# Two transformer blocks in one kernel: another way to the head norms, other places for gains, first scores, rank strips and small loads

## The chip, the cores and the metric

One NeuronCore of a Trainium2 chip. The metric is the device time of the kernel in microseconds, the median of several runs. Matmuls have float32 data; where the text says "product", it is one of three terms (hi by hi, hi by lo, lo by hi) of a split float32 product.

## What is computed

Two blocks, one after the other, on x of 512 tokens by 1024. Only the first is touched by the change. Cut to what matters:

```python
h = rms_norm(x, g_norm)
proj = h @ w_in          # q_a k_a v_a q_i k_i w_i z_a c_q c_kv k_rope z_b q_m z_m gates
q_a = partial_rope(rms_norm(q_a.reshape(b, s, 8, 64), g_qn_a), cos_a, sin_a)   # k_a likewise, g_kn_a
o_a = dsa_attention(q_a, k_a, v_a, q_i, k_i, w_i)       # an indexer picks the best 128 keys per query
q_b = (rms_norm(c_q, g_cq) @ w_uq).reshape(b, s, 8, 96)
kv_b = (rms_norm(c_kv, g_ckv) @ w_ukv).reshape(b, s, 8, 128)
k_b = concatenate([k_nope, broadcast(k_rope)])
q_b, k_b = rms_norm(q_b, g_qn_b), rms_norm(k_b, g_kn_b)  # then rotate the last 32 of 96
o_b = causal_attention(q_b, k_b, v_b)
kv_m = rms_norm(mem, g_mem) @ w_mem_kv                   # mem: 256 rows
k_m, q_m = rms_norm(k_m, g_kn_m), rms_norm(q_m, g_qn_m)  # 4 heads of 128
o_m = softmax(q_m k_m / sqrt(128)) v_m
ys = [o_a * silu(z_a), o_b * silu(z_b), o_m * silu(z_m)]
x = x + (sum_n sigmoid(gates_n) * (ys_n @ w_branch_n)) @ w_out
```

The second block (pool mixer, sparse attention, MLP of 4096) follows and takes the time from about 700 us on.

## The kernel before, in words

**Strips and pairs.** The large products run in strips on TensorE (PE). A strip has 4 PSUM banks and takes its weights in pairs: 2 x 128 rows of up to 512 columns. SP loads a pair into one of 4 ring slots (`raw`) once the pair four before is used (`load`, L457 on), ACT makes the high part (`part_hi`, L1356), POOL the low part (`split`, L606), PE uses it in `strip_products` (L777). Before each of the eight steps kt of a strip, PE may do small work given as `before` (transposes of 128x128 pieces, called groups, and first scores). A group takes a bank that the group two before it has been emptied from, by ACT ("A"), DVE ("D") or both, as `GROUPS` says; cq and ckv are "AD".

**Order of strips.** Strips 0 to 5, 7, 8, 10, 11 are the ten of `w_in` (`in1(0)` to `in1(9)`, 484 columns), strips 6 and 9 the two of the memory (512 columns, two token tiles, 4 x 12 products), 12 is gate strip 0, then stage a of attention, 13 and 14 the q ranks (`STRIP_UQ`), 15 and 16 the kv ranks (`STRIP_UKV`), 17 gate strip 1, stages b0, b1, m, and the merge strips. Each engine's program is written out by hand in this order; nothing is planned at run time.

**Start.** ACT issues the load of the identity and nine loads of small vectors into `vec_rows` (L1351), PE turns them (L726) into `vec`, then turns x (`turn_x`, four pieces at first), ACT makes xt_hi (L1385), DVE xt_lo. ACT then issues nine more small loads (L1471 to L1477) and only then the first w_hi (L1356).

**Head norms.** DVE squares and reduces q_a and k_a (L1951, L1952), forms the mean (L1969), POOL raises it to -0.5 (`inv_sqrt`, L600), DVE multiplies by the factor (L1958) and by the gain (L1959) and rotates. The same follows for the memory keys, ranks and q_m, with a second POOL power. For branch b the factor comes from ACT's root and a Newton step on DVE (`roots` L1639, `over_rms` L2270 to L2274), for all 8 heads at once behind both kv strips. POOL has the power between `split`s in its program.

**The place of the waits.** In in1(9), PE's `a_columns` at kt 2 waits for `z_ready` 2 and `qk_ready`; at kt 6 it turns z_a. In gate strip 0, `b_columns` turns z_b at kt 1 and z_m at kt 3 (`turn_z`, 16 transposes), waits for `cq_ready` at kt 5 and turns the ranks at kt 5 to 7; scores of units 0 and 1 follow. `silu(n)` (L2104) is DVE's, after ACT's tanh (`gate_tanh`, L1447). After the strip DVE scales the four gate banks (`scale_gates1`, L2256), and PE waits for it (`strip_scaled`) before the attention stage. DVE's program has silu(2) and two head scalings ahead of the low parts of the cq and ckv groups (L2249).

**Attention.** A stage works in steps of two units (a head and a block of 128 queries). Per step: scores (PE, L839), mask and maximum (DVE, L2168), exponential (ACT, L1590), reciprocal (DVE, L2189), scaling (POOL, L639), transposes (PE, L974) `LAG_T` steps later, copies (DVE L2196 for even units, ACT L1602 for odd ones), product with v (PE, L982). `AHEAD` is the number of steps whose scores stand before the stage.

**Behind stage m**, ACT copies o_a's part to ys_hi (L1707), DVE subtracts it (L2386, ys_lo), and the merge strips start.

## Time and profile before

| | |
|---|---|
| runs | 1604.28 us median of 3 (1604.19 to 1605.44) |
| the profiled execution's own time | 1605.06 us |
| its span | 1603.2 us |
| granted clock, mean | 0.969 |

The profile is of one execution. The page gives busy times of the engines over the span, the span in 40 slices, the chain of waits that ended last, and groups of instructions by line; further views give PE's instructions in order of time with the idle time ahead of each and what ended it, a table of waits, and the busy time and granted clock in chosen stretches. A busy share says little here: what counts is where PE stands, and what it stands for. "PE bank L777 x12" is twelve products of a strip.

### The profile page before, as it was taken

How to read it: one execution, taken by the hardware profiler on the slowest of the kernel's cores; microseconds unless marked ns; L12 is line 12 of the kernel's file. 1: busy time of each engine (PE TensorE's matmuls, PEld its weight loads, DVE VectorE, ACT ScalarE, POOL GpSimd, SP SyncE). 2: the span in 40 equal slices, each digit the busy share in tenths (PEclk: the TensorE clock that was granted, in tenths of full speed). 3: DMA queues.
4: the chain of work that ended last, by engine and by line, in shares of the span. 5: the costliest groups of instructions: out<-in, count | busy, mean ns of one | idle time of the engine just before them, and what ended most of it. 6: DMA issues, size and time to landing. Idle time of an engine off the chain costs nothing.

```text
span 1603.2 us, 20921 instructions
## 1 busy us (share of the span) xinstructions
PE 1510.6 (94%) x7906; PEld 1251.9 (78%) x7906; DVE 675.1 (42%) x1382; ACT 601.5 (38%) x1081; POOL 672.3 (42%) x448
## 2 busy tenths in 40 slices
PE   5999977999787999999999889999999999999998
PEld 4888866858556888889988677877888888888886
DVE  2336959564654122410316536565122333323324
ACT  3454431556355132333223527465322422222222
POOL 2433575434341344444333226353444444444443
PEclk8999998999998999999999979899999999999999
DMA  5222332102100323336522200002222222322322
GB/s 170 87 77 87 115 114 63 55 16 83 49 1 1 92 92 105 113 118 199 153 83 66 66 27 2 1 2 79 94 101 94 89 99 92 103 94 92 104 92 92
DMA packets 72426, 130.70 MB, mean 82 GB/s; under 512 B 5961, under 2 KB 28818, under 8 KB 72338
## 3 DMA queue, kind: packets, MB, share of 16 engines
q1 hardware_dynamic: 69968, 127.01, 24.7%
q10 hardware_dynamic: 2370, 2.50, 0.5%
q8 instruction: 58, 0.95, 0.2%
q14 instruction: 30, 0.25, 0.1%
HBM read 125.29 MB, written 4.19 MB: 81 GB/s over the span
## 4 chain that ended last, share of the span: by engine, by line
PE 88%; DVE 4%; ACT 3%; POOL 2%; issue 2%; DMA 1%; ACTq 0%; DVEq 0%; POOLq 0%
PE bank L777 68%; PE bank L982 4%; PE bank L839 4%; PE bank L974 4%; PE bank L726 3%; PE bank L992 1%; PE bank L841 1%; PE bank L1150 1%; POOL w_lo L606 1%; POOL rstd L600 1%; ACT w_hi L1356 1%; PE bank L1014 0%; PE bank L1315 0%; DMA vec_rows<-in_pe_v 0%; DVE q_parts L2064 0%
## 5 line engine op out<-in xcount | busy, mean ns | idle before, releaser
L606 POOL TENSOR_TENSOR w_lo<-raw,w_hi 128x1024 fp32r<-128x1024 f32 (+3 forms) x222 | 528.1, 2381 | 740.3 <-ACT w_hi L1356 740.3
L1356 ACT ACTIVATE w_hi<-raw 128x1024 fp32r<-128x1024 f32 (+3 forms) x222 | 226.5, 1023 | 640.8 <-DMA raw<-in_w_ff 255.0
L777 PE MATMUL bank<-w_hi,xt_hi 128*128 128x484 f32 (+2 forms) x640 | 242.2, 378 | 18.3 <-POOL w_lo L606 18.3
L777 PE MATMUL bank<-w_lo,xt_hi 128*128 128x484 f32 (+2 forms) x640 | 238.8, 373 | 0.0
L777 PE MATMUL bank<-w_hi,xt_lo 128*128 128x484 f32 (+2 forms) x640 | 238.7, 373 | 0.0
L777 PE MATMUL bank<-xt_hi,w_hi 128*128 128x512 f32 x576 | 227.0, 394 | 1.0 <-issue 1.0
L777 PE MATMUL bank<-xt_hi,w_lo 128*128 128x512 f32 x576 | 224.6, 390 | 0.0
L777 PE MATMUL bank<-xt_lo,w_hi 128*128 128x512 f32 x576 | 224.5, 390 | 0.0
L777 PEld LDWEIGHTS bank<-w_hi,xt_hi 128*128 128x128 f32 x640 | 121.7, 190 | 34.4 <-issue 19.7
L777 PEld LDWEIGHTS bank<-w_hi,xt_lo 128*128 128x128 f32 x640 | 121.5, 190 | 15.2
L777 PEld LDWEIGHTS bank<-w_lo,xt_hi 128*128 128x128 f32 x640 | 121.8, 190 | 14.3
L777 PEld LDWEIGHTS bank<-xt_hi,w_hi 128*128 128x128 f32 x576 | 108.3, 188 | 23.4 <-issue 1.7
L777 PEld LDWEIGHTS bank<-xt_hi,w_lo 128*128 128x128 f32 x576 | 108.2, 188 | 22.7
L777 PEld LDWEIGHTS bank<-xt_lo,w_hi 128*128 128x128 f32 x576 | 108.3, 188 | 22.2 <-issue 0.5
L777 PE MATMUL bank<-w_hi,ys_hi 128*128 128x512 f32 x240 | 93.5, 390 | 0.0
L777 PE MATMUL bank<-w_hi,ys_lo 128*128 128x512 f32 x240 | 93.5, 389 | 0.0
L777 PE MATMUL bank<-w_lo,ys_hi 128*128 128x512 f32 x240 | 93.5, 389 | 0.0
L1590 ACT ACTIVATE sc<-sc,negmax 128x128 f32<-128x128 f32 (+3 forms) x112 | 56.6, 506 | 64.2 <-DVE negmax L2168 64.0
L726 PE MATMUL bank<-cst,proj 128*128 128x128 f32 (+2 forms) x368 | 54.9, 294 | 26.0 <-issue 10.2
L2517 DVE SCALAR_TENSOR_TENSOR proj<-bank,r_rows 128x512 f32<-128x512 f32 x32 | 19.9, 684 | 140.8 <-PE bank L777 140.8
L726 PEld LDWEIGHTS bank<-cst,proj 128*128 128x128 f32 (+2 forms) x368 | 45.2, 148 | 35.7 <-issue 27.1
L2356 DVE TENSOR_TENSOR proj<-proj,bank 128x512 f32<-128x512 f32 x56 | 34.7, 682 | 69.7 <-PE bank L777 69.7
(335 smaller groups left out, 2412.9 us busy)
## 6 DMA issues: line engine op xcount, KB each, us to landing
raw<-in_w_ff SPq DMA_DIRECT2D x64, 512.0 KB, 3.5
raw<-in_w_in SPq DMA_DIRECT2D x40, 512.0 KB, 3.4
raw<-in_w_in SPq DMA_DIRECT2D x40, 484.0 KB, 3.4
raw<-in_w_in SPq DMA_DIRECT2D x24, 392.0 KB, 3.3
raw<-in_w_out SPq DMA_DIRECT2D x16, 512.0 KB, 3.6
raw<-in_w_branch SPq DMA_DIRECT2D x12, 512.0 KB, 3.6
raw<-in_w_mem_kv SPq DMA_DIRECT2D x8, 512.0 KB, 3.6
raw<-in_w_proj_nsa SPq DMA_DIRECT2D x8, 512.0 KB, 3.5
```

Of the source, the lines that this page charges most:

```text
L600: pool.tensor_tensor(rstd[:, 0:n], stat[:, 0:n], half[:, 0:n], ALU.pow).then_inc(sem["pow_done"], 1)
L606: pool.tensor_tensor(w_lo[:, slot, 0:halves, 0:width], raw[:, slot, 0:halves, 0:width], w_hi[:, slot, 0:halves, 0:width].bitcast(F32), ALU ...
L726: ins = pe.transpose(b[0:m, o:o + k], src, ident[0:k, 0:k])
L777: ins = pe.matmul(o, lhs, rhs, start=st and j == 0, stop=en and j == 2)
L839: ins = pe.matmul(o, w["q"], w["k"], start=True, stop=w["k_lo"] is None)
L841: ins = pe.matmul(o, w["q"], w["k_lo"], start=False, stop=True)
L974: ins = pe.transpose(bank[2 + u % 2][0:n, t * P:(t + 1) * P], src[:, t * P:t * P + n], ident)
L982: ins = pe.matmul(bank[4 + w["pas"] % 2][w["rows"], w["cols"]], w["v"][t], src[0:n, t * P:(t + 1) * P], start=w["start"] and t == 0, stop= ...
L1356: act.activation(w_hi[:, slot, 0:halves, 0:width], raw[:, slot, 0:halves, 0:width], ACT.Copy)\
L1590: act.activation(v, v, ACT.Exp, scale=-1.0, bias=negmax[:, u % SC:u % SC + 1], accum_out=sums[:, u % SC:u % SC + 1]).then_inc(sem["exps"], 1)
L2356: ins = dve.tensor_tensor(v, v, banks[t][:], ALU.add)
L2517: ins = dve.scalar_tensor_tensor(relu[:, m, :], banks[m][:], 0.0, r_rows[:], ALU.max, ALU.mult)
```

## The change

(1) Squares of heads are ACT's, and all head norms go by ACT's root and DVE's Newton step; POOL's powers over 64 and 32 columns are gone. (2) Head gains are applied where ACT (for b1's keys DVE) empties the transposed groups; for the rotated dimensions they are multiplied into the angles (`gained_a`, `gained`). (3) The two memory strips are 6 and 7, in1(6) to in1(8) strips 8 to 10. (4) In in1(9) the q and k groups start at kt 3; in gate strip 0 the rank groups start at kt 1; z_b and z_m are turned in gate strip 1. (5) Scores of units 0 to 3 of stages a and b0 are made inside the gate strips, and the gates are scaled inside the stage, in two halves. (6) Rank strips go q, kv, q, kv, and branch b's norms run for four heads after each pair of them. (7) ys of branch a is made inside stage m. (8) Small loads go from ACT's queue to SP's, x comes in three loads instead of two.

```diff
-AHEAD = {"a": 1, "b0": 1, "b1": 0, "m": 0, "n": 2}
+AHEAD = {"a": 2, "b0": 2, "b1": 0, "m": 0, "n": 2}
-IN1_AT, IN1_COL, MEM_AT = (0, 1, 2, 3, 4, 5, 7, 8, 10, 11), (3, 4, 0, 1, 2, 5, 6, 7, 8, 9), (6, 9)
+IN1_AT, IN1_COL, MEM_AT = (0, 1, 2, 3, 4, 5, 8, 9, 10, 11), (3, 4, 0, 1, 2, 5, 6, 7, 8, 9), (6, 7)
...
@@ score_bank
+            if u in (2, 3):
+                return bank[u]
+            if u - b0 in (2, 3):
+                return bank[2 + u - b0]
...
@@ SP
+            x_load(0, 256, "x_in")
...
             in1_load(0, 0)
+            x_load(256, 256, "x_in2")
+            in1_load(0, 1)
+            x_load(S, S, "x_rest")
+            in1_load(0, 2)
+            in1_load(0, 3)
+            sp.dma_start(pos_i[:], positions[0].rearrange("(t p) -> p t", p=P), allow_slow_non_contiguous=True)\
+              .then_inc(sem["pos_in"], 16)
             sp.dma_start(cst[:, P:EARLY], cst_d[:, P:EARLY]).then_inc(sem["cst_in"], 16)
+            for src in (norm_mix_2[0].rearrange("(r c) -> r c", c=P), norm_mlp_2[0].rearrange("(r c) -> r c", c=P),
...
+                sp.dma_start(vec_b[r:r + src.shape[0], :], src).then_inc(sem["vec_in"], 16)
+                r += src.shape[0]
+            sp.wait_ge(sem["half_set"], 1)
...
+                sp.dma_start(vec_b[r:r + 1, c:c + src.shape[1]], src).then_inc(sem["gains_in"], 16)
             sp.dma_start(proj[:, 0:2, 2792:2792 + D], mem[0].rearrange("(t p) d -> p t d", p=P)).then_inc(sem["mem_in"], 16)
+            for dst, src in rows.values():
+                sp.dma_start(dst[:], src.to_broadcast(dst.shape)).then_inc(sem["row_in"], 16)
...
@@ POOL
-            inv_sqrt(64)
...
-            inv_sqrt(32)
...
@@ PE, in1(9): a_columns
-                if kt == 2:
+                if kt == 3:
                     strip_left(10)
-                    pe.wait_ge(sem["z_ready"], 2)
                     pe.wait_ge(sem["qk_ready"], 1)
...
@@ PE, gate strip 0
-            def b_columns(kt):
+            def rank_columns(kt):
                 if kt == 1:
                     strip_left(11)
-                    turn_z(1, 0)
-                if kt == 3:
-                    turn_z(2, 0)
-                if kt == 5:
-                    pe.wait_ge(sem["zt_emptied"], 12)
                     pe.wait_ge(sem["cq_ready"], 1)
                     for k in range(2):
                         group("cq", k, columns(CQ + P * k))
-                if kt == 6:
+                if kt == 2:
                     group("cq", 2, columns(CQ + P * 2))
                     group("ckv", 0, columns(CKV))
-                if kt == 7:
+                if kt == 3:
                     group("ckv", 1, columns(CKV + P))
+                if kt == 5:
+                    emptied("ckv", 1)
                     scores(0)
                     scores(1)
+                if kt == 6:
+                    scores(2)
+                    scores(3)
...
@@ PE, attention
+                    entry = {"a": (STRIP_GATE0, 3, 4, 1), "b0": (STRIP_GATE1, 2, 3, 2)}.get(stage)
+                    if entry and step == p0 + entry[1]:
+                        pe.wait_ge(sem["gate_half"], entry[3])
+                    if entry and step == p0 + entry[2]:
+                        strip_scaled(entry[0])
...
@@ PE, gate strip 1: first_heads
+                if kt == 1:
+                    strip_left(STRIP_UKV + 2)
+                    turn_z(1, 4)
+                if kt == 2:
+                    pe.wait_ge(sem["zt_emptied"], 8)
+                    pe.wait_ge(sem["b_ready"], 1)
+                if 2 <= kt <= 5:
+                    head_columns(0, kt - 2)
                 if kt == 6:
+                    emptied("b0", 7)
+                    turn_z(2, 4)
+                if kt == 7:
+                    pe.wait_ge(sem["zt_emptied"], 12)
+                    for u in range(u_b, u_b + 4):
+                        scores(u)
...
@@ ACT, start
+            for q in range(4):
+                for k in (2 * q, 2 * q + 1):
+                    turned_hi(0, k, VEC["norm"])
+                in1_hi(q)
...
@@ ACT, strips 6 to 12
             empty_mem(0)
+            act.wait_ge(sem["emptied_a"], strips_emptied("A", MEM_AT[0]))
+            act.wait_ge(sem["ix_acc"], 24)
+            act.activation(sq_km[:], kvm[:, :, 0:S], ACT.Square).then_inc(sem["sq_made"], 1)
             for p in range(31, 35):
                 in1_hi(p)
+            empty_mem(1)
+            in1_hi(35)
+            act.wait_ge(sem["emptied_a"], strips_emptied("A", IN1_AT[4]))
+            head_squares()
+            for p in range(36, 39):
+                in1_hi(p)
             empty_in1(6)
...
+            rank_squares()
...
             empty_in1(7)
             gate_tanh(1, ZB, 7)
...
+            in1_hi(43)
+            roots(0, stat, 64)
...
+            to_rows("q", 0, q_t)
+            to_rows("q", 1, q_t)
+            roots(1, stat2, 32)
...
             turned_z(0, ZA, 4)
             empty_in1(9)
...
             next_hi(PAIR_GATE0 + 3, S)
...
             for k in range(2):
                 ranks_hi("cq", k, cq_hi)
+            gate_tanh(2, ZM, 9)
+            ranks_hi("cq", 2, cq_hi)
...
@@ ACT, behind stage a (squares are made behind each empty_uq and empty_ukv)
+            next_hi(PAIR_UKV, S)
+            part_hi(PAIR_UQ + 3, (PAIR_UQ + 3) % RING, 2, 384)
             act.wait_ge(sem["o_emptied"], STAGE_PASSES["a"][1])
             act.activation(yt["ya"], proj[:, :, ZA:ZA + S], ACT.Copy).then_inc(sem["y_moved"], 1)
             empty_uq(0)
+            part_hi(PAIR_UQ + 4, (PAIR_UQ + 4) % RING, 1, 384)
+            next_hi(PAIR_UKV + 3, S)
+            empty_ukv(0)
+            next_hi(PAIR_GATE1, S)
+            roots(2, stat, 32)
             empty_uq(1)
             next_hi(PAIR_GATE1 + 1, S)
             next_hi(PAIR_GATE1 + 2, S)
             empty_ukv(1)
             next_hi(PAIR_GATE1 + 3, S)
+            turned_z(1, ZB, 4)
+            roots(3, stat, 32)
             act.preload_act_table(ACT.Exp)
             for h in range(4):
+                head_gain(0, h, "q")
+                head_gain(0, h, "k")
+                if h in (1, 3):
+                    next_hi(PAIR_MERGE + 8 + h // 2, S)
+            turned_z(2, ZM, 4)
...
@@ ACT, stage m
+                        act.activation(ys_a[0][:, t, :], proj[:, t, YTA:YTA + S], ACT.Copy).then_inc(sem["ysa_hi"], 1)
...
@@ DVE, behind the top-k
+            dve.wait_ge(sem["sq_made"], 2)
+            head_sums(sq_a[:], 0, 16, stat)
+            mean_of(stat, 0, 64, 64).then_inc(sem["mean_made"], 1)
             silu(0)
+            head_sums(sq_km[:], 0, 4, stat2)
...
+            over_rms(0, stat, 64)
+            head_scale(heads(QA, 16, 64), 16, 64, 0)
...
             dve.sem_inc(sem["qk_ready"], 1)
             silu(1)
...
+            over_rms(1, stat2, 32)
...
             dve.sem_inc(sem["cq_ready"], 1)
+            head_scale(kvm[:, :, 0:512].rearrange("p t (h d) -> p t h d", h=4), 4, P, 0)
+            head_scale(heads(QM, 4, P), 4, P, 16)
             silu(2)
...
@@ DVE, scale_gates1
+                for m in (2, 3, 0, 1):
                     ins = dve.tensor_tensor(g(m), banks[m][:], r_rows1[:], ALU.mult)
+                    if m == 3 and first_half:
+                        ins.then_inc(sem["gate_half"], 1)
...
@@ DVE, stage m
+                        dve.tensor_tensor(ys_a[1][:, t, :], proj[:, t, YTA:YTA + S], ys_a[0][:, t, :].bitcast(F32), ALU.subtract)\
+                           .then_inc(sem["ysa_lo"], 1)
```

## Rows read from the trace of the kernel before

**Rows 1.** Part 1 of the page: busy time of the engines.
```profile
PE 1510.6 (94%) x7906; PEld 1251.9 (78%) x7906; DVE 675.1 (42%) x1382; ACT 601.5 (38%) x1081; POOL 672.3 (42%) x448
```

**Rows 2.** PE's instructions in order of time: start, length; in brackets the idle time ahead.
```profile
10.12 0.36 PE L726 MATMUL bank<-cst,vec_rows 73*128 73x73 f32 x1 [10.12 <-DMA vec_rows<-in_pe_v]
22.14 0.74 PE L777 MATMUL bank<-w_hi,xt_hi 128*128 128x484 f32 x1 [8.65 <-POOL w_lo L606]
...
240.63 0.74 PE L777 MATMUL bank<-w_hi,xt_hi 128*128 128x484 f32 x1 [9.64 <-POOL w_lo L606]
279.33 0.87 PE L726 MATMUL bank<-cst,proj 128*128 128x128 f32 x3 [10.20 <-issue]
...
338.49 0.63 PE L974 MATMUL bank<-cst,sc 128*128 128x128 f32 x4 [0.80 <-DVE prob_t L2196]
...
415.51 3.85 PE L726 MATMUL bank<-cst,proj 128*96 128x128 f32 x16 [5.60 <-DVEq L2300]
...
436.69 1.02 PE L974 MATMUL bank<-cst,sc 128*128 128x128 f32 x6 [0.19 <-POOL sc L639]
...
515.62 0.77 PE L777 MATMUL bank<-ys_hi,w_hi 128*128 128x512 f32 x1 [5.50 <-DVE ys_lo L2386]
```

**Rows 3.** The table of waits, PE: us in total, times, longest.
```profile
PE bank L839 <- DVE mix L2256: 5.5, 2, 2.8
```

**Rows 4.** Stretches: busy us of PE, PEld, DVE, ACT, POOL; granted clock; DMA.
```profile
0.00:516.00 516.00, 446.89 (x2414) 365.34 (x2415) 291.43 (x597) 233.66 (x441) 222.97 (x156) 0.95 0.23 71
220.00:240.00 20.00, 10.99 (x49) 8.71 (x47) 2.08 (x2) 10.39 (x12) 17.29 (x4) 0.87 0.42 126
345.00:382.00 37.00, 36.26 (x300) 28.09 (x299) 16.87 (x62) 21.13 (x56) 14.30 (x23) 1.00 0.10 31
```

**Rows 5.** The chain of waits in order of time: start, us, what.
```profile
22.14 7.53 PE bank L777 x24
...
34.05 23.61 PE bank L777 x108
...
240.63 23.27 PE bank L777 x96
...
279.33 1.94 PE bank L726 x8
281.27 3.31 PE bank L777 x12
...
295.06 1.75 PE bank L726 x16
...
415.51 3.85 PE bank L726 x16
...
515.62 4.61 PE bank L777 x10
```

**Rows 6.** ACT's first w_hi, and ACT's first load: KB, us to landing.
```profile
18.36 1.91 ACT L1356 ACTIVATE w_hi<-raw 128x968 fp32r<-128x968 f32 x2 [4.02 <-issue]
...
cst<-cst_d ACTq DMA_DIRECT2D x1, 64.0 KB, 2.8
```

**Rows 7.** POOL in order of time, at the power.
```profile
227.74 10.56 POOL L600 TENSOR_TENSOR rstd<-stat,half 128x64 f32<-128x64 f32 x1
```

**Rows 8.** Part 6 of the page: loads of pairs, KB, us to landing.
```profile
raw<-in_w_in SPq DMA_DIRECT2D x40, 512.0 KB, 3.4
```

**Rows 9.** DVE in order of time: a scaling, a silu, a step of 32 columns.
```profile
238.34 4.30 DVE L1958 TENSOR_TENSOR proj<-proj,rstd 128x2048 f32<-128x2048 f32 x1 [17.92 <-POOL rstd L600]
...
306.39 2.29 DVE L2104 SCALAR_TENSOR_TENSOR proj<-proj 128x2048 f32<-128x2048 f32 x1 [6.25 <-ACT proj L1447]
...
393.47 2.39 DVE L2274 TENSOR_TENSOR rstd<-rstd,stat 128x32 f32<-128x32 f32 x1
```

**Rows 10.** ACT in order of time, at its first tanh.
```profile
168.30 1.28 ACT L1447 ACT_TABLE_LOAD   x1
169.60 1.92 ACT L1447 ACTIVATE z_tanh<-proj 128x2048 f32<-128x2048 f32 x1
```

More of the change, by code:

```diff
@@ L285, in two_block_kernel @@
         gained = place("gained", [P, 4, TT, 16], where=top[0])
+        gained_a = place("gained_a", [P, 8, TT, 8], where=top[0])
         r_cols = place("r_cols", [P, TT, P], where=top[0])
@@ L861, in memory_rows @@
                     strip_left(0)
+                    pe.wait_ge(sem["vec_in"], 16 * 7)
+                    pe.wait_ge(sem["gains_in"], 16 * 8)
+                    group("vec2", 0, transposes([(vec_b[:, :], 63, P)]))
                     pe.wait_ge(sem["mem_in"], 16)
@@ L1501, in _ @@
             in1_hi(8)
+            b = group_wait("vec2", 0)
+            act.activation(vec[:, 16:79], b[:, 0:63], ACT.Copy).then_inc(sem["group_a"], 1)
             memory_hi(0)
@@ L1613, in attention @@
                         act.activation(probs_c[:, :, 0:P], o, ACT.Copy).then_inc(sem["cmp_copied_a"], 1)
+                    if stage == "m" and step - p0 in (3, 4, 5, 6):
+                        t = step - p0 - 3
+                        if t == 0:
+                            act.wait_ge(sem["o_emptied"], STAGE_PASSES["b1"][1])
+                        act.activation(ys_a[0][:, t, :], proj[:, t, YTA:YTA + S], ACT.Copy).then_inc(sem["ysa_hi"], 1)
                     if nsa and step - p0 in (8, 12):
@@ L2181, in attention @@
                         take_compressed(g, (2, 3))
+                    if step == p0 + AHEAD[stage] and stage == "a":
+                        scale_gates1(STRIP_GATE0, lambda m: mix2[:, m, :], first_half=True)
+                    if step == p0 + AHEAD[stage] and stage == "b0":
+                        scale_gates1(STRIP_GATE1, lambda m: mix2[:, 4 + m, :], first_half=True)
                     if p0 + AHEAD[stage] <= step < p1:
```

477 lines of the change are left out of this document (222 added, 255 removed), and 4 rows, old and new, of the table GROUP_OF.

## The prediction

> **What bounds the kernel now.** Part 1 of the page [rows 1]: TensorE (PE) is busy 94% of the span, every other engine under half. So the time is PE's work plus the holes in it, and I read PE's own timeline for holes above 2 us. Before 520 us it shows 8.65 us ahead of the first product, 9.64 at 231, 10.20 at 269, 5.60 at 410 and 5.50 at 510, each with what ended it [rows 2]; the table of waits adds two of 2.74 and 2.79 (5.5 in all), both for DVE's scaling of a gate strip, at 330 and 428 [rows 3]. After 520 us holes that long stand only in code that isn't touched. Then the granted clock, in stretches [rows 4]: 0.87 round the 9.64 us hole, 0.95 over the first 516 us, 1.00 in the steady part of stage a, where PE hardly stops. A hole is thus paid twice, and the chain of waits has the second price [rows 5]: 108 products at full clock take 23.61 us (0.219 each), so 96 take 21.0; behind the 9.64 us hole 96 took 23.27 (2.3 more), the first 24 took 7.53 instead of 5.25 (2.3), 16 transposes behind the 5.60 us one 3.85 instead of the 1.75 of others (2.1), ten products behind the 5.50 us hole 4.61 instead of 2.28 (2.3); behind the 10.20 us hole transposes and 12 products lose 1.1 and 0.7. That is 2.4 GHz against 1.2 after PE has stood for 5 us or more.
>
> **The change part by part.** Times are those of before, relative to the landmark named. Durations come from one execution of 1605.06 us (span 1603.20), 0.8 above the median of 1604.28; I carry differences over unchanged.
>
> *1. Start.* PE's first transpose waits until 10.12 for the last of nine small loads on ACT's queue [rows 2]; ACT then issues nine more, and is idle 4.02 us for that alone in front of its first w_hi at 18.36 [rows 6]. After, ACT issues three loads ahead of it, by about 2.2 us. Landing is bounded by 2.8 us (the identity's load [rows 6]) and the 5.2 that the last row load took: first transpose at 5 to 7.4, I take 6.1. Before, it took 12.0 us from there to the first product; now four instead of nine steps stand between: vec copy and two turned tiles to +2.8, w_hi 1.0, w_lo 2.3, handshakes: 6.5. First product at 12.6 instead of 22.14: **-9.5** (-8.2 to -10.6). The slow phase behind it I leave as it is. The moved loads are 20 on SP's queue, plus one from cutting x in two: 21 x 0.45 us, about 9.5 us, done by 16 us, ahead of SP's next issue, which waits for PE to free a slot (29.7 before, 20 after). If that cover went, SP would be late by what sticks out, and four loaded pairs still stand between.
>
> *2. Head norms without POOL's power.* POOL's pow over 64 columns takes 10.56 us in front of the w_lo on which PE waits [rows 7]. It goes to ACT's root and five small DVE steps: the 9.64 us hole and its 2.3 of clock go, **-11.9**. The root itself and its table load lie in strip 10, beside PE's products (part 3 has their cover). Both memory strips in a row need a pair per 2.74 us; a load lands in 3.4 [rows 8], w_hi 1.06 and w_lo 2.4 add up to 7.1 with handshakes, under three pairs' time (8.2), so I put 0 (up to 1 more).
>
> *3. qk_ready.* The 10.20 us hole is DVE's chain: rank squares, KR and silu(1) stand ahead of what PE asks for at kt 2. Scaling 2048 columns took 4.30 us beside POOL's subtractions, a pass of 2048 columns alone takes 2.29 [rows 9], and each of q and k was passed over twice. Now root 0 stands on ACT behind empty_in1(7), a tanh and w_hi 43: 6.8 us into strip 10. From there: Newton step 1.7, scaling 4096 columns in one pass with POOL in between 6.6, two rotations 7.2: qk_ready about 1 us into strip 11, PE asks 7.9 us into it. Cover 6.9 us. The hole goes with its clock: **-12.0**.
>
> *4. A new wait in gate strip 0.* DVE's program still has silu(2) ahead of the cq/ckv low parts, and group cq2 needs group cq0 emptied by DVE too. Formerly ranks came at kt 5; now at kt 1. Count from the end of strip 11: ACT empties it (2.3), w_hi 51 lands at 3.5 and ends at 4.5, two rank copies to 5.8; then tanh(2), 1.92 us, and because ACT's last table is now the root's, a table load, 1.28 [rows 10]: 9.0. Silu(2) 2.29 [rows 9] to 11.3, low part of cq0 0.75: 12.1. PE has done kt 0, two groups and kt 1 by 6.35. Hole 5.8, and 2.2 of clock as behind its like: **+8.0** (0 to +10). The load itself reads 168.30 to 169.60 with the tanh directly behind it. The Trainium skill (ScalarE: Activation LUTs, "What ACT_TABLE_LOAD costs") adds a drain of about 1.38 us to every switch, 2.66 in all; by that this term would be +9.4. The trace has no such drain at this load.
>
> *5. turn_z(1), turn_z(2)* leave gate strip 0 and come back in gate strip 1, 16 transposes of 1.75 us together [rows 5], twice, in either place: 0.
>
> *6. Entry of stage a.* From the end of the strip to the transposes of units 2 and 3 it is 8.2 us: hole 2.74 [rows 3], slow scores, 0.80 for a copy [rows 2]. After: DVE scales the gates to 2.6, masks units 4 and 5 to 3.8, 6 and 7 to 5.1, copies unit 0 by 5.65, which frees the transposes. -2.5; scores of 2 and 3 sit in the strip (+0.6), those of 8 and 9 are done earlier (-0.4): **-2.3**.
>
> *7. Rank strips interleaved.* The four strips cost the same in any order, 23.7 us. Norms of the first half start after UKV0, 11.9 us in. Chain: squares 15.0, reduction and mean 16.7, root 17.9, scaling, rotation and keys with three of POOL's subtractions in the way (one 32-column step lasted 2.39 in such a meeting [rows 9]): b_ready 1 at 29.5 to 31; PE asks at 31.0. So the 5.60 hole, its 2.1 and 0.3 behind it go, -8.0. The second half's norms now stand in front of ACT's Exp load and the first head_gain: +2.0 (0 to 6): **-6.0**.
>
> *8. Entry of b0.* End of strip to the transposes of units 4 and 5 it is 9.5 us [rows 2], after: 7.5 (gate half 1.4, scores 1.5, scores of 6 and 7 1.9, norms by POOL). Strip +1.7 for four scores: **-0.3**.
>
> *9. ys of branch a inside stage m.* Behind m stand ACT's ys_hi and DVE's ys_lo, 2048 columns each and as long as tanh and silu [rows 9, 10]: the 5.50 us hole, and 2.3 of clock [rows 2, 5]. After, PE waits only for the last o_emptied (0.9): -6.9. Four ACT copies of 0.57 and four DVE subtractions of 0.7 enter steps of 2.2 us, of which ACT has some 1.65 busy: 2.25, so +1.0 (0 to 2.5). **-5.9**.
>
> *10. Gains.* Gains at evictions replace copies on ACT; row passes on DVE are dropped off the path: 0, hidden by PE's products. Two more angle products in front of the memory rows are covered by 4 us of DVE waiting.
>
> Sum: -9.5 -11.9 -12.0 +8.0 -2.3 -6.0 -0.3 -5.9 = **-39.9 us**. 1604.28 - 39.9 = **1564.4**; the profiled execution would be 1565.2.
>
> **The rivals.**
> *B. The wait in gate strip 0 doesn't show* (tanh(2) earlier than I count, ACT idle then): 1556.4. For it: all the rest is as above. Against: the order of both programs has it. 0.15.
> *C. The start gives less.* The small rows land as late as before since x and w saturate the 16 DMA engines: first transpose at 10.1, start -5.5: 1568.4. Against: they are issued ahead of the others. 0.12.
> *D. The stalls move instead of going.* Behind the rank strips ACT and DVE alternate (root, table, gain), POOL blocks DVE's two-input steps, and 7 gives only 0 to -2, stage m +2.5: 1571. For: margins of 0 to 1 us at b_ready 1. 0.20.
> *E. Slower: the clock.* Roots, gates and scores leave PE many 2 to 5 us waits in the first 516 us instead of three long ones. PE is busy 447 us there at a mean clock of 0.95 [rows 4]. The stretch round the 9.64 us hole shows 0.87; were the whole 447 us at 0.86, it would lengthen by 447 x (0.95/0.86 - 1) = 47 us: 1611. It decides from 0.87, where it has eaten the gain. Against: stage a's steady part, full of small gaps, has 1.00 [rows 4]. 0.02.
> *F. The change does little of what it says:* roots on ACT come so late (behind w_hi 43) that qk_ready misses kt 3 by as much as before: 1576. 0.05.
>
> **How the numbers follow.** Forecast 0.46, B 0.15, C 0.12, D 0.20, F 0.05, E 0.02. Bounds of the main case: -8.2 to -10.6 at the start, 0 to +10 in gate strip 0, 0 to 6 in part 7, 0 to 2.5 in m; they don't all fall on one side. B, C and D lie inside 1552 to 1575, with 4 us past B and D; outside stay F, E and the ends where bounds add up. A change of 0.2% (3.2 us) is about what a measurement of this kernel can tell from none. Faster 0.96, same 0.015, slower 0.025 (E, and a little for a stall of 40 us and more that I don't see).
>
> **What would show it.** PE's first product near 12.6; no hole on POOL's rstd in strip 10; none before the first aq group; a hole of about 6 us ending on DVE's rank low part in gate strip 0; transposes of units 2 and 3 under 6 us behind that strip; gate strip 1 without a hole over 2 us; under 1 us between stage m and the merge strips. Wrong it is if mean clock falls, if a hole over 3 us stands in the memory strips or at aq, or if anything behind 520 us changes its length.

## The result and the profile after

The changed kernel takes **1566.07 us** (median of 4 runs, 1563.63 to 1566.45) against 1604.86 for the kernel before (4 runs, 1604.19 to 1606.05): ratio 0.9754, 95% interval 0.9737 to 0.9771. That is 38.8 us less; forecast were 39.9 less, 1564.4. The profiled execution of the changed kernel took 1566.19 us, its span 1564.4 at a mean clock of 0.984 (before: 1603.2 at 0.969).

Part 1 of the page answers to [rows 1]. PE does the same number of instructions in 6 us less, the slow clock that went, and its share of the span rose from 94% to 96%; the rest of the gain is holes (time in which PE stands).

```profile
PE 1504.5 (96%) x7907; PEld 1244.9 (80%) x7907; DVE 656.7 (42%) x1385; ACT 618.8 (40%) x1115; POOL 650.4 (42%) x446
```

PE's own timeline, in the columns of [rows 2]:

```profile
6.11 0.28 PE L757 MATMUL bank<-cst,vec_a 16*128 16x16 f32 x1 [6.11 <-DMA cst<-cst_d]
12.67 0.74 PE L808 MATMUL bank<-w_hi,xt_hi 128*128 128x484 f32 x1 [2.67 <-POOL w_lo L640]
...
281.82 1.94 PE L757 MATMUL bank<-cst,proj 128*128 128x128 f32 x8 [5.76 <-DVE projr L2338]
307.91 0.63 PE L1006 MATMUL bank<-cst,sc 128*128 128x128 f32 x4 [1.19 <-ACT prob_t L1662]
374.50 1.05 PE L757 MATMUL bank<-cst,proj 128*96 128x128 f32 x8 [2.57 <-DVEq L2376]
379.98 1.22 PE L757 MATMUL bank<-cst,proj 128*96 128x128 f32 x8 [1.68 <-ACT q_t L1711]
...
480.40 0.70 PE L808 MATMUL bank<-projr,w_hi 128*128 128x512 f32 x2 [0.94 <-issue]
```

Of the long holes of before, those of 9.64 and 10.20 us have no counterpart at all: between 166.63 and 276 PE never waits 0.25 us. The 5.50 us in front of the merge strips are 0.94. The 5.60 us in gate strip 1 are 2.57 and 1.68. One hole is new, 5.76 us in gate strip 0. The clock, by stretches in the columns of [rows 4]: slow round that new hole and behind the entry of stage a, then full to the end of stage m.

```profile
281.82:286.85 5.03, 5.03 (x20) 4.38 (x21) 2.01 (x3) 2.11 (x3) 1.55 (x1) 0.71 0.00 0
302.54:312.38 9.84, 7.37 (x41) 4.01 (x40) 7.28 (x27) 5.20 (x18) 4.17 (x8) 0.83 0.13 40
308.00:313.00 5.00, 5.00 (x30) 3.06 (x30) 1.92 (x10) 3.14 (x12) 2.76 (x6) 0.66 0.00 0
312.00:480.00 168.00, 150.27 (x1032) 114.05 (x1028) 98.16 (x268) 100.12 (x243) 63.45 (x82) 1.00 0.10 30
```

Cut both timelines at the same places of the work, and the 38.8 us fall as follows (length after less length before; the forecast column gathers the prediction's terms for that stretch, the 32 transposes of step 5 included):

| stretch | measured | forecast |
|---|---|---|
| start to the first product (22.14, 12.67) | -9.5 | -9.5 |
| to the last weight pair of the first memory strip (175.07, 166.63) | +1.0 | 0 |
| to the end of gate strip 0 (330.31, 302.62) | -19.3 | -18.8 |
| to units 2 and 3 (338.49, 307.91) | -2.9 | -2.9 |
| rest of stage a (369.91, 340.86) | +1.5 | 0 |
| rank strips, gate strip 1 (427.22, 399.79) | +1.6 | -0.8 |
| to units 4 and 5 of b (436.69, 406.30) | -3.0 | -2.0 |
| rest of b0 and b1 (489.13, 457.74) | -1.0 | 0 |
| stage m (515.62, 480.40) | -3.8 | -3.6 |
| merge strips to the first product behind the second block's attention (1112.84, 1073.97) | -3.7 | -2.3 |
| rest | +0.1 | 0 |

So the sum was right to 1.1 us. The experiments ask whether the terms were also right for the reasons given. They undo or vary parts 2, 4, 7, 9 and 10 of the prediction; the start (part 1) and the entries of the stages (parts 6 and 8) rest on the traces alone, and so does most of part 3.

### The profile page after: what moved, and what is told of

Read it like the earlier page. It is cut to its first block, busy times and chain, and to the rows that moved or that the text cites. A ratio compares the mean times of both kernels' runs of the same rounds, so it can differ in the third digit from the quotient of the medians.

```text
span 1564.4 us, 20973 instructions
## 1 busy us (share of the span) xinstructions
PE 1504.5 (96%) x7907; PEld 1244.9 (80%) x7907; DVE 656.7 (42%) x1385; ACT 618.8 (40%) x1115; POOL 650.4 (42%) x446
## 4 chain that ended last, share of the span: by engine, by line
PE 90%; DVE 4%; ACT 3%; issue 2%; POOL 1%; DMA 1%; DVEq 0%; ACTq 0%; POOLq 0%
PE bank L808 70%; PE bank L1014 4%; PE bank L870 4%; PE bank L1006 4%; PE bank L757 2%; PE bank L1024 1%; PE bank L872 1%; PE bank L1191 1%; PE bank L1046 0%; ACT w_hi L1391 0%; PE bank L1356 0%; DVE q_parts L2156 0%; DVE mix L2404 0%; DMA cst<-cst_d 0%; POOL w_lo L640 0%
## 5 line engine op out<-in xcount | busy, mean ns | idle before, releaser
L640 POOL TENSOR_TENSOR w_lo<-raw,w_hi 128x1024 fp32r<-128x1024 f32 (+4 forms) x222 | 521.0, 2349 | 723.2 <-ACT w_hi L1391 723.1
L1391 ACT ACTIVATE w_hi<-raw 128x1024 fp32r<-128x1024 f32 (+4 forms) x222 | 226.4, 1022 | 611.4 <-DMA raw<-in_w_ff 254.6
L1650 ACT ACTIVATE proj<-proj,negmax 128x512 f32<-128x512 f32 (+2 forms) x80 | 49.6, 620 | 37.7 <-DVE negmax L2248 37.4
```

Source lines behind the costliest of these rows:

```text
L640: pool.tensor_tensor(w_lo[:, slot, 0:halves, 0:width], raw[:, slot, 0:halves, 0:width], w_hi[:, slot, 0:halves, 0:width].bitcast(F32), ALU ...
L1391: act.activation(w_hi[:, slot, 0:halves, 0:width], raw[:, slot, 0:halves, 0:width], ACT.Copy)\
L1650: act.activation(v, v, ACT.Exp, scale=-1.0, bias=negmax[:, u % SC:u % SC + 1], accum_out=sums[:, u % SC:u % SC + 1]).then_inc(sem["exps"], 1)
```

## The experiments

Each run was timed beside the kernel before. To set a run against the changed kernel (ratio 0.9754) I use two figures: its ratio times 1605, and in its profile the time from the end of PE's first 24 products to the first product of the merge strips, 459.6 us in the changed kernel (480.40 - 12.67 - 8.17). That leaves out what the start and the late stages do from one execution to the next.

| run | median, us | ratio, 95% interval | against the change, by ratio | 24 products to merge |
|---|---|---|---|---|
| changed kernel | 1566.07 | 0.9754, 0.9737 to 0.9771 | | 459.6 |
| silu_late | 1557.15 | 0.9705, 0.9692 to 0.9718 | -7.9 | 451.4 |
| no_meet | 1561.74 | 0.9727, 0.9713 to 0.9740 | -4.3 | 456.9 |
| pow_back | 1567.42 | 0.9773, 0.9758 to 0.9788 | +3.0 | 461.2 |
| ys_back | 1575.64 | 0.9811, 0.9796 to 0.9826 | +9.1 | 463.2 |
| rank_order | 1568.40 | 0.9752, 0.9717 to 0.9787 | -0.3 | 464.1 |
| two_loads | 1567.71 | 0.9758, 0.9724 to 0.9792 | +0.6 | 462.1 |
| no_meet_gain | 1562.22 | 0.9719, 0.9696 to 0.9743 | -5.6 | 454.9 |
| all4 | 1556.18 | 0.9687, 0.9667 to 0.9707 | -10.8 | 449.6 |
| before_mem67 | 1603.56 | 0.9972, 0.9953 to 0.9990 | | 483.6 |
| before_root | 1598.72 | 0.9945, 0.9921 to 0.9969 | | 480.8 |

The kernel before has 486.0 in the last column (515.62 - 22.14 - 7.53).

### silu_late: the new wait in gate strip 0

```
             head_scale(heads(QM, 4, P), 4, P, 16)
-            silu(2)
...
                     dve.scalar_tensor_tensor(parts[1][:, k, :], b[:], vec[:, VEC[v] + k:VEC[v] + k + 1],
                                              parts[0][:, k, :].bitcast(F32), ALU.mult, ALU.subtract)\
                        .then_inc(sem["group_d"], 1)
+            silu(2)
```

> The changed kernel with one DVE step moved: the gating of z for branch m (silu(2)) stands behind the low parts of the five rank groups instead of ahead of them. Theory: the 5.76 us hole of TensorE at 281.82 in gate strip 0 is DVE waiting in program order for ACT's table load (1.28) and tanh (1.91) and its own 2.29 pass. With the low part of cq0 free to follow ACT's copy it is done by about 275.9, before PE asks at 276.06. What is left is cq2's copy on ACT, which stands behind the tanh (free at 278.63): under 1 us of hole. Strip end 302.62 to about 295.8; with the slow products behind the hole (1.07 + 0.6 us) 6 to 7.4 us less in all, near 1559.5. Rival 1, the hole is paid once only: 5 us, 1561. Rival 2, the wait is ACT's and not DVE's: the hole stays above 3 us, gain under 3, 1564. Rival 3, the slow stretch behind the entry of stage a (309.0 to 312.5) belongs to that earlier hole and goes too: 1.7 us more, 1558.

The chain of waits of the changed kernel shows the wait as the prediction counted it: two rank copies, table load, tanh, DVE's pass, low part.

```profile
274.24 1.16 ACT projr L1519 x2
...
275.41 1.28 ACT L1482
276.71 1.92 ACT z_tanh L1482
...
280.93 0.76 DVE projr L2338
...
281.82 1.94 PE bank L757 x8
283.76 3.25 PE bank L808 x12
```

PE's timeline of silu_late, and a stretch of it with the granted clock:

```profile
279.02 0.63 PE L757 MATMUL bank<-cst,proj 128*128 128x128 f32 x4 [0.30 <-DVE projr L2336]
```
```profile
278.00:305.00 27.00, 24.23 (x130) 16.61 (x130) 13.91 (x45) 10.30 (x33) 7.76 (x12) 1.00 0.13 42
```

The 5.76 us are gone; 0.30 us is what is left. The stretch is 8.2 us shorter: 5.5 of hole, 1.7 of slow products behind it (8 transposes in 1.94 us and 12 products in 3.25, where others take 0.87 and 2.63), and 1.5 at the entry of stage a, where the slow phase does not come in this run (clock 1.00 where the changed kernel had 0.66 for 5 us); some 0.5 is given back in small pieces. The theory holds for the hole. Rival 3, that the slow phase at the entry belongs to it, is not shown. Seven traces of this study have a hole of 5.7 us or more in gate strip 0. In four of them (changed kernel, pow_back, ys_back, two_loads) the transposes and 12 products behind it took 5.0 to 5.2 us and the entry of stage a, up to its third group of scores, 9.8; in the other three (no_meet, no_meet_gain, rank_order) they took 6.4 to 6.5 and 8.3. For no_meet:

```profile
281.77:288.20 6.43, 6.43 (x20) 5.37 (x21) 2.01 (x3) 2.11 (x3) 1.83 (x1) 0.54 0.00 0
303.90:312.22 8.32, 5.86 (x41) 3.10 (x40) 7.18 (x27) 4.73 (x17) 3.79 (x7) 1.00 0.17 47
```

Both add up to 3 us more than without a slow phase, so in every one of the seven the hole went with its length and 3 us more, spent at once or half of it some 25 us later. But all4 (below), which has no hole there, had the slow entry of 9.8 us again, so 1.5 of silu_late's gain may be chance.

### two_loads: what a table load costs there

```
+            act.preload_act_table(ACT.Exp)
+            act.preload_act_table(ACT.Sqrt)
             gate_tanh(2, ZM, 9)
```

> The changed kernel with two table loads more on ACT in front of the tanh in gate strip 0 (to Exp's table and back to the root's), nothing else. Theory: a load takes 1.28 us and nothing stands round it, so the tanh starts 2.56 us later, the hole at 281.82 grows from 5.76 to 8.3 and the time by 2.6 to 3.5 us (with a longer slow stretch): near 1569. Rival, each switch also drains ACT for about 1.38 us, 2.66 in all (the Trainium skill, ScalarE: Activation LUTs, What ACT_TABLE_LOAD costs): the tanh starts 5.3 us later, hole 11.1, time 5.3 to 6.5 us longer, near 1572.

ACT in order of time, then PE:

```profile
274.50 1.28 ACT L1634 ACT_TABLE_LOAD   x1
275.79 1.28 ACT L1635 ACT_TABLE_LOAD   x1
277.08 1.28 ACT L1482 ACT_TABLE_LOAD   x1
278.38 1.91 ACT L1482 ACTIVATE z_tanh<-proj 128x2048 f32<-128x2048 f32 x1
```
```profile
283.49 1.94 PE L757 MATMUL bank<-cst,proj 128*128 128x128 f32 x8 [8.35 <-DVE projr L2340]
```

Three loads stand back to back at 1.29 us each and the tanh follows at once. The hole grew by 2.59 us, twice a load, and the stretch by 2.5: no drain. The Trainium skill (ScalarE: Activation LUTs, "What ACT_TABLE_LOAD costs") has 1283 ns for the load, as here, and about 1380 ns of drain on top of every switch to a different set; the rows show nothing of that. Over the whole run 0.6 us by ratio and 1.6 by median are left of it, within the interval.

### pow_back, before_mem67, before_root: whose hole was the one of 9.64 us?

```
 # pow_back, on the changed kernel
-            for s in range(2, 12):
+            for s in range(2, 10):
                 split_strip(s)
+            pool.wait_ge(sem["mean_made"], 1)
+            pool.tensor_tensor(rstd[:, 0:64], stat[:, 0:64], half[:, 0:64], ALU.pow).then_inc(sem["root_made"], 1)
+            split_strip(10)
+            split_strip(11)
-            roots(0, stat, 64)            # ACT
-            over_rms(0, stat, 64)         # DVE
+            dve.wait_ge(sem["root_made"], 1)
```

> The changed kernel with POOL's power back for the first 64 columns (ahead of the subtractions of strip 10), and without ACT's first root and DVE's five Newton steps. Theory (term 2 of the prediction): POOL is held about 10.5 us, TensorE stands about 9.6 us in front of strip 10 and runs slow for about 2.3 us behind it: 11.9 us longer, near 1578. qk_ready comes no later against PE, so nothing is added at the first aq group. Rival 1, the loads and the two memory strips now leave more pairs in hand and hide a part: under 8 us, 1574. Rival 2, the later qk_ready also holds up the aq groups: over 14 us, above 1580.

The theory and rival 2 fell. Rival 1 had the mechanism, more pairs in hand, but not the size: it put 1574, and 1567.4 came. The power is back, as long as ever, and costs PE two waits of 0.17 and 0.93 us. PE, then POOL, in order of time:

```profile
221.49 0.46 PE L812 MATMUL bank<-w_hi,xt_hi 128*128 128x484 f32 x1 [0.17 <-POOL w_lo L640]
227.90 0.46 PE L812 MATMUL bank<-w_hi,xt_hi 128*128 128x484 f32 x1 [0.93 <-POOL w_lo L640]
```
```profile
208.50 10.60 POOL L697 TENSOR_TENSOR rstd<-stat,half 128x64 f32<-128x64 f32 x1
...
221.30 6.45 POOL L640 TENSOR_TENSOR w_lo<-raw,w_hi 128x968 fp32r<-128x968 f32 x1
```

The power begins at 208.50, 12.8 us before PE wants the first pair of strip 10 (221.49 - 0.17 = 221.3). In the kernel before it began at 227.74 [rows 7], 3.3 us before PE wanted that pair (240.63 - 9.64 = 231.0). Power and subtraction less the lead give the hole both times: 10.6 + 2.3 - 3.3 is the 9.6 us of before, 10.6 + 2.2 - 12.8 leaves nothing. The 0.93 us stand in front of the next pair, whose subtraction took 6.45 us instead of 2.3: it lies under DVE's scaling of 4096 columns (two inputs, 219.21 to 225.63). So it was not the power's length that decided but the lead that POOL had, and that came from another part of the change, costed at 0: the memory strips had stood at 6 and 9, the second of them right ahead of the power. Four pairs of a memory strip last 2.74 us each, 11 us in all; four of strip 9 as it is now last 21. About 8 us of either go for loading, copying and subtracting the last of them. To see each part by itself, I took them alone on the kernel before:

```
 # before_mem67
-IN1_AT, IN1_COL, MEM_AT = (0, 1, 2, 3, 4, 5, 7, 8, 10, 11), (3, 4, 0, 1, 2, 5, 6, 7, 8, 9), (6, 9)
+IN1_AT, IN1_COL, MEM_AT = (0, 1, 2, 3, 4, 5, 8, 9, 10, 11), (3, 4, 0, 1, 2, 5, 6, 7, 8, 9), (6, 7)
 # ... and loads, products and evictions in that order
```

> The kernel before with one part of the change: the two memory strips stand in a row at 6 and 7 instead of at 6 and 9 (loads, products and evictions in that order). POOL's power over 64 columns stays where it is, ahead of the subtractions of strip 10. Theory, formed on the run with the power put back, which cost 1.3 us where I had 11.9: what made the power cost 9.64 us was that it stood behind a memory strip, whose pairs last 2.74 us each, so that POOL had only some 8 us of pairs in hand; with pairs of 5.25 us in front of strip 10 it has some 15. The 9.64 hole and the 2.3 us of slow products go with no root at all. The power ends near 229 instead of 238.3, 9.5 earlier, while PE comes to strip 11 11.9 earlier, so the hole at the aq groups grows from 10.20 to about 12.5. In all 9 to 10 us less: near 1595. Rival, the prediction's step 2 (the power holds POOL wherever it stands): hole stays near 9.6, time within 2 us of 1604.9.

```
 # before_root
-            inv_sqrt(64)                                          # POOL
             in1_hi(39)                                            # ACT
+            act.wait_ge(sem["mean_made"], 1)
+            act.activation(rstd[:, 0:64], stat[:, 0:64], ACT.Sqrt).then_inc(sem["root_made"], 1)
 # ... DVE: mean, then 1/r and one Newton step in place of the wait for POOL
```

> The kernel before with one part of the change: the first 64 columns get ACT's root (behind the copy of pair 39) and five Newton steps on DVE in place of POOL's power; the memory strips stay at 6 and 9. Theory: POOL's subtraction for pair 40 follows ACT's copy at once, done near 230.3 where PE asks at 231.0, so the 9.64 us hole and its 2.3 us go; rstd is ready near 228.5 instead of 238.3, 9.8 earlier, PE comes 11.9 earlier, the aq hole grows by 2. In all 9.5 to 10 us less: near 1595. With the run before that would mean that either part alone empties the hole, and the two together give it once. Rival, ACT has no room there (its copy of pair 39 stands behind an eviction and a tanh): the table load and the root push pair 40's copy to 229 or later and a hole of 2 us or more stays: 1597 or above.

PE's timeline of before_mem67, with its POOL, and PE's of before_root:

```profile
233.74 0.46 PE L776 MATMUL bank<-w_hi,xt_hi 128*128 128x484 f32 x1 [2.65 <-POOL w_lo L605]
272.11 1.94 PE L725 MATMUL bank<-cst,proj 128*128 128x128 f32 x8 [10.32 <-issue]
```
```profile
218.87 12.53 POOL L599 TENSOR_TENSOR rstd<-stat,half 128x64 f32<-128x64 f32 x1 [0.48 <-DVE stat L1968]
```
```profile
269.04 1.94 PE L725 MATMUL bank<-cst,proj 128*128 128x128 f32 x8 [11.56 <-issue]
```

In before_mem67 the power begins 12.2 us ahead of PE (it now waits for DVE's mean), lasts 12.5 and leaves 2.65 us of hole (12.5 + 2.3 - 12.2 = 2.6); in before_root there is none. Up to the aq groups the two are 7.2 and 10.3 us ahead of the kernel before. Either part alone takes most of the hole, and the other then brings next to nothing. The hole at the aq groups stays in both (10.32 and 11.56), so the 12.0 us of the prediction's step 3 come from neither of these parts. In all three kernels with the hole, q and k were rotated before PE stood there (266.2 against 269.1 in the kernel before, 259.2 against 261.8 in before_mem67, 256.8 against 257.5 in before_root), and the hole ended 0.3 to 0.4 us behind silu(1): at kt 2 PE also waits for `z_ready` 2. DVE in the kernel before, the last step of the rotations and silu(1):

```profile
265.74 0.41 DVE L1981 TENSOR_TENSOR proj<-junk 128x256 f32<-128x256 f32 x1
...
276.73 2.29 DVE L2104 SCALAR_TENSOR_TENSOR proj<-z_tanh,proj 128x2048 f32<-128x2048 f32 x1
```

The change drops that wait and shortens DVE's chain as well. Dropping the wait alone, the cheaper edit, was not tried.

The whole runs gained less than that: 4.5 and 8.8 us by ratio (2.2 and 7.0 by median), where 9 to 10 were expected. At the end of stage m before_mem67 is only 2.4 us ahead (last column). Stretches of 14 us from the entry of stage a, kernel before, then before_mem67:

```profile
333.00:347.00 14.00, 13.16 (x94) 7.29 (x94) 9.04 (x40) 9.36 (x32) 6.04 (x13) 0.88 0.00 0
```
```profile
326.00:340.00 14.00, 13.31 (x70) 7.61 (x72) 7.45 (x34) 7.99 (x27) 5.57 (x12) 0.63 0.00 0
```

The same work with the same holes ran at 0.63 instead of 0.88 and did 70 PE instructions where it had done 94. Its ten runs spread from 1596.87 to 1606.95, the seven of before_root from 1593.55 to 1603.87. Why the slow phase is longer there was not settled.

### no_meet and rank_order: why the first half of branch b was still late

In the changed kernel DVE and POOL, in order of time (b_ready 1 follows the step that ends at 374.09):

```profile
357.38 2.42 DVE L2361 TENSOR_TENSOR stat<-stat,kr_sq 128x16 f32<-128x16 f32 x1
...
364.40 2.63 DVE L2039 TENSOR_TENSOR rot_b<-proj,gained 128x256 f32<-128x256 f32 x1
367.06 2.49 DVE L2040 TENSOR_TENSOR proj<-rot_b 128x256 f32<-128x256 f32 x1
369.48 2.62 DVE L2041 TENSOR_TENSOR proj<-rot_b 128x256 f32<-128x256 f32 x1
```
```profile
357.36 2.41 POOL L640 TENSOR_TENSOR w_lo<-raw,w_hi 128x1024 fp32r<-128x1024 f32 x1 [2.91 <-ACT w_hi L1391]
364.35 7.46 POOL L640 TENSOR_TENSOR w_lo<-raw,w_hi 128x1024 fp32r<-128x1024 f32 x3 [4.58 <-ACT w_hi L1391]
```

DVE's four slow steps lie under POOL's four subtractions, one each, and end with them. Alone such steps take 0.19 to 0.43 us.

```
             for p in range(PAIR_UKV + 3, PAIR_MERGE + 10):
+                if p == PAIR_GATE1 + 2:
+                    pool.wait_ge(sem["b_ready"], 1)
                 split(p, p % RING, 2, S)
```

> The changed kernel with one wait more on POOL: its subtractions for the third and fourth weight pair of gate strip 1 start only when the first half's q and k of branch b are ready (b_ready 1). Theory: b_ready 1 comes at 374.1 instead of by 371.9 because DVE's two-input steps lie still while POOL subtracts: four of them read 2.42 to 2.63 instead of 0.19 to 0.43 and 1.23. Two of the four meetings (367.06 and 369.48) go: b_ready 1 near 370.2, the 2.57 us hole at 374.50 goes, the 1.68 one at 379.98 shrinks by at most the same shift or stays; time 2.5 us less, near 1563.7. Rival: the steps are slow for another reason (the length of the rows, a bank), then 367.06 and 369.48 stay at 2.5 us, b_ready 1 stays at 374.1 and the time is unchanged or, since the late pairs now hold up gate strip 1 at its kt 4, 1 to 3 us longer.

DVE of no_meet, then POOL:

```profile
357.43 2.36 DVE L2024 TENSOR_SCALAR stat<-stat 128x32 f32<-128x32 f32 x1
...
366.85 0.42 DVE L2042 TENSOR_TENSOR proj<-rot_b 128x256 f32<-128x256 f32 x1
367.19 0.42 DVE L2043 TENSOR_TENSOR proj<-rot_b 128x256 f32<-128x256 f32 x1
...
371.54 1.22 DVE L2013 TENSOR_REDUCE stat<-sq_k 128x16 f32<-128x1024 f32 x1
372.79 1.72 DVE L2363 TENSOR_TENSOR stat<-stat,kr_sq 128x16 f32<-128x16 f32 x1
```
```profile
369.73 4.75 POOL L640 TENSOR_TENSOR w_lo<-raw,w_hi 128x1024 fp32r<-128x1024 f32 x2 [3.19 <-DVEq L2378]
```

Two meetings went, q and k of the first half were ready at 369.6, and the 2.57 us hole is gone; the next, 1.71 us for ACT, stayed. The stretch is 2.7 us shorter, the theory's 2.5. By ratio the run gained 4.3. The rows also show which steps are held: an addition of 16 columns (357.38) and a one-input tensor_scalar (357.43 in no_meet) wait until POOL is through, a reduction of 1024 columns in the midst of POOL's work keeps its 1.22. The Trainium skill (SBUF — State Buffer, "Who interferes with whom") has it so: a DVE step with two inputs in SBUF, or in a mode that takes the second port pair, fully blocks against a GpSimd step that reads SBUF, a tensor_reduce never. The trace agrees for the two-input additions (2.42 us) and the reduction (1.22); the tensor_scalar was held as well (2.36), but no row shows its mode.

```
 # rank_order: both q strips, then both kv strips, on all engines; the two tables that change:
-    48, 52, 54, 58, 54, 90, 98, 122, 150, 158)
+    48, 52, 56, 58, 54, 90, 98, 122, 150, 158)
-    12, 13, 14, 17, 16, 28, 30, 36, 44, 46)
+    12, 13, 15, 17, 16, 28, 30, 36, 44, 46)
```

> The changed kernel with the rank strips in the order of before (both q strips, then both kv strips), squares of a half as soon as its strips are out. Theory (term 7): the first half's kv squares come 6 to 6.5 us later, b_ready 1 at 380 instead of 374.1, the hole at 374.50 grows from 2.57 to 8.7, and behind it 16 transposes and 12 products run slow (about 2.2 us): 8 us longer, near 1574. Rival, the meetings with POOL fall elsewhere: if POOL has finished gate strip 1's pairs before the rotation, b_ready 1 is only 2 to 4 us later and the time 2 to 4 us longer.

PE's timeline:

```profile
371.33 1.96 PE L757 MATMUL bank<-cst,proj 128*128 128x128 f32 x16 [3.28 <-ACT proj L1703]
378.88 1.05 PE L757 MATMUL bank<-cst,proj 128*96 128x128 f32 x8 [2.82 <-DVEq L2381]
```

With the order of before q and k of the first half come 4.4 us later (378.88 instead of 374.50), not 6 or more. The hole in front of them hardly grew, because a new one stands ahead, 3.28 us for ACT's eviction of the last kv strip, which stands behind the second half's squares. The stretch is 4.5 us longer, in between theory and rival; over the whole run the ratio shows nothing, with an interval of 5.6 us either way. The interleaving is thus worth some 4.5 us here, not 8.

### no_meet_gain: the gains ahead of the second root

```
             for h in range(4):
                 head_gain(0, h, "q"); head_gain(0, h, "k")
+                if h == 0:
+                    roots(3, stat, 32); act.preload_act_table(ACT.Exp)
-            roots(3, stat, 32); act.preload_act_table(ACT.Exp)    # had stood ahead of the loop
```

> The changed kernel with POOL's wait of the run no_meet, and on ACT the gains of the first head (its q and k) ahead of the second half's root and of the load of Exp's table, instead of behind them. Theory: with b_ready 1 no longer late, the 1.7 us hole at the second head's transposes (377.04 in no_meet) is ACT standing in the root's wait and the 1.28 us load while the first head's banks are full. It goes; nothing comes in its place, since the root then stands behind one head and the next head's copies come 3.5 us later. 1.7 us below no_meet, 1.5 to 3 with the clock: near 1559.5. Rival, the wait comes back one head later with the same length (root and load now ahead of the second head's copies): 1561.7 as no_meet.

Behind the entry of stage a no hole of 0.9 us or more is left up to the hole at 396.84, and the stretch is 2.0 us shorter than in no_meet (454.9 against 456.9): the theory. The median is no lower than no_meet's; 1.3 us by ratio lie inside the intervals.

### ys_back: branch a's split behind stage m

```
-                        act.activation(ys_a[0][:, t, :], proj[:, t, YTA:YTA + S], ACT.Copy).then_inc(sem["ysa_hi"], 1)
-                        dve.tensor_tensor(ys_a[1][:, t, :], proj[:, t, YTA:YTA + S], ys_a[0][:, t, :].bitcast(F32), ALU.subtract)\
 # behind attention("m"), on ACT and on DVE
+                    act.activation(ys_a[0], yt[name], ACT.Copy).then_inc(sem["ysa_hi"], 1)
+            dve.tensor_tensor(ys_a[1], proj[:, :, YTA:YTA + S], ys_a[0].bitcast(F32), ALU.subtract)\
```

> The changed kernel with the split of branch a's output back behind stage m: ACT's copy and DVE's subtraction of 2048 columns each, both after the last step of the stage, instead of four quarters inside it. Theory (term 9): a hole of 5.5 us between stage m and the merge strips instead of 0.94, ten slow products behind it (2.3 us), and the steps of stage m 1.0 us shorter in sum: 5.9 us longer, near 1572. By the two traces the stage alone was 3.83 us shorter and what lies behind 2.2 us: 6.0. Rival, the four quarters cost stage m 2.5 us: 4.4 us longer, 1570.5, with stage m's length down by 2.5.

```profile
484.52 1.19 PE L808 MATMUL bank<-projr,w_hi 128*128 128x512 f32 x2 [5.47 <-DVE projr L2379]
```

The hole is back with 5.47 us, and the stretch up to its end 3.6 longer. The whole run is 9 us longer, though, where 5.9 were expected: 2.6 more come at once behind the hole, slow products, and the rest 400 us on, in code that is the same in all kernels here. Stretches there, changed kernel and then ys_back:

```profile
892.00:900.00 8.00, 8.00 (x31) 6.95 (x31) 0.79 (x3) 0.00 (x0) 0.00 (x0) 0.57 0.01 2
```
```profile
896.00:911.00 15.00, 15.00 (x62) 13.74 (x62) 2.05 (x8) 0.37 (x2) 0.12 (x1) 0.54 0.02 2
```

PE is busy without a break in both; the slow phase lasts some 7 us in one and 14 in the other.

### all4: everything together

```
 # silu_late + no_meet + no_meet_gain, and on ACT's queue:
-            g_norm's rows, identity, g_mem's rows
+            identity, g_norm's rows, g_mem's rows
```

> Everything of the runs silu_late, no_meet and no_meet_gain together, and the identity's load issued ahead of the norm rows at the start. Theory: the gains add, since each hole stands at a place of its own: 8.9 (gating behind the ranks' low parts), 4.3 (POOL's wait), 1.7 (gains ahead of the root) off 1566.1; the identity's load brings 0 to 0.6, since the memory's norm row, still issued third, lands at about 6.3 us as well. Near 1551, no hole over 1.5 us between the first product and stage n. Rival 1: part of the 8.9 and 4.3 was the same slow clock counted twice (silu_late took a slow stretch at the entry of stage a with it, no_meet shortened one too): 1553 to 1555. Rival 2, a new hole: gate strip 1 comes 14 us earlier and its loads or POOL's halves are late: 1556 or above.

1556.18 us, ratio 0.9687: 3.1% below the kernel before and some 10 below the changed one. It is the fastest kernel of this study, though silu_late alone is not told apart from it. Between the first product and the merge strips no hole above 1.4 us is left, as expected, so rival 2 falls although its 1556 is met; the time lies 1 us above the 1553 to 1555 of rival 1. PE's clock in all4:

```profile
300.00:306.00 6.00, 5.42 (x31) 3.27 (x32) 2.54 (x17) 3.90 (x15) 3.24 (x6) 0.72 0.00 0
306.00:437.00 131.00, 122.81 (x833) 92.53 (x834) 76.83 (x210) 82.08 (x189) 55.61 (x66) 1.00 0.13 39
437.00:442.00 5.00, 4.13 (x36) 3.26 (x35) 0.69 (x1) 0.60 (x1) 0.00 (x0) 0.66 0.00 0
```

The slow phase at the entry of stage a, which silu_late was rid of, is back, and a short one in stage b1 besides. So all4 is 10.0 us shorter to the merge strips, where the three gains add to 12.9 (8.2, 2.7 and 2.0). The two slow phases are the difference: 1.5 us at the entry of stage a, which silu_late's trace did not have, and 1.4 in stage b1, which none of the three had. That is slow clock that comes in one trace and not in another, rather than the same clock counted twice, as rival 1 had it. The identity's load brought nothing: PE's first transpose waits until 6.40 for g_mem's row.

## Why the prediction was right, and where it was not

The forecast held in time and in sign (38.8 against 39.9). That it came within 1.1 us is in part luck: by the table above, four stretches came out 5.0 us dearer than forecast and five 4.1 us cheaper, and part 2 was right in size for a reason that does not hold alone. Step by step:

1. *Start, -9.5.* Right to 0.1 us (12.67 against 12.6), with the steps as counted; SP's small loads were issued by 16.0. No run undoes this part. Over nine kernels with this start the first transpose came at 6.11 to 6.49. Rival C (landing as late as before) fell. The slow phase that I left unchanged was 0.6 longer: 24 products in 8.17 us instead of 7.53 [rows 5].
2. *POOL's power, -11.9.* The hole went, and the time is right; **this is the step that failed as a reason**. "It goes to ACT's root: the 9.64 us hole goes" gave the root a gain that the order of the memory strips, costed at 0, brings by itself: with the power put back 1.1 us of waits come back. What I read was the power's length; what I did not ask was how many microseconds of pairs POOL had in hand when it began (3.3 before, 12.8 in pow_back).
3. *qk_ready, -12.0.* Right in size. No wait at the aq groups, and neither the root nor the strips alone takes that hole. q and k were ready 5.1 us before PE asked (246.0 and 251.2) instead of 6.9: scaling and rotations took 4.4 and 10.6 us, where I had 6.6 and 7.2. With POOL's power in pow_back they were ready at 240.5, so ACT's root is no help here. And what PE stood for was silu(1) and not q and k; whether the shorter chain or the dropped wait takes the hole is open, since either would do by the rows.
4. *New wait in gate strip 0, +8.0.* Right: 5.76 us for 5.8, released by the step that I named. The slow part was 1.7 instead of 2.2 right behind it, and another 1.5 at the entry of stage a, which I had put nowhere and which is not surely this hole's. Rival B fell. The table load without a drain was right.
5. *Transposes moved, 0.* As forecast, no trace of a cost.
6. *Entry of stage a, -2.3.* The way to units 2 and 3 was right (5.3 us for 5.65), but 1.5 was given back in the stage by the slow phase named in step 4. With the +0.6 that stands in the strip, the part comes to about -0.8.
7. *Rank strips, -6.0.* Mis-sized by 2.4. q and k of the first half were ready at 374.1, 33.2 us behind stage a's end, where I had "29.5 to 31": four meetings with POOL instead of three, each to its full length, on steps of 0.19 to 0.43 us. Holes of 2.57 and 1.68 where I allowed 2.0 for both. Rival D had this mechanism, but a third of its size.
8. *Entry of b0, -0.3.* It was 1 us better than forecast (6.5 us to units 4 and 5 for 7.5), and 1.4 more of slow clock went that stood in b0 before.
9. *ys of branch a, -5.9.* Right: stage m -3.8 for -3.6, and 2.2 behind it.
10. *Gains, 0.* Nothing on PE's path.

My sign of being wrong, "if anything behind 520 us changes its length", did come: the stretch from the merge strips to the end of the second block's attention is 3.7 us shorter, 1.4 more than the forecast for it; for the same 3346 instructions PE was busy 3.1 us less and idle 0.6 less, so it is slow clock in the main. Rivals E and F have nothing for them: the mean clock rose, and no aq wait is left.

## What to carry over

In these traces a long step on a helper engine cost the main engine its length, and that of the step behind it, less the lead that the helper had when it began; so read the start of the step against the time at which the next result is wanted, and count what a reordering does to the size of the items in between. Where two edits of one change can each take the same hole, their gains don't add, and only taking or undoing them one at a time shows it. Where a wait is for several things, read which of them ended it: at the aq groups it was not the one that the step was named for. Steps of DVE with two inputs on a critical chain should be costed with a full subtraction of POOL's for every one that can meet them, however short they are.
